# Activation buffers of a two-block network kernel laid out on multiples of 128 bytes in SBUF

## What is computed

```
h = rmsnorm(x, norm1_g[l]) * (1 + sc1) + sh1
x = x + g1 * hybrid_mixer(h, ...)
h = rmsnorm(x, norm2_g[l]) * (1 + sc2) + sh2
x = x + g2 * ((silu(h @ Wg) * (h @ Wu)) @ w_ffn_out[l])
```

## The kernel before, in words

| buffer | used for | begins at (before) | past a multiple of 128 |
|---|---|---|---|
| `weights_hi`, `weights_lo` | stationary operand | 65664, 82048 | 0, 0 |
| `h_hi`, `h_lo` | moving, first block | 107744, 124128 | 96, 96 |
| `rope_cos`, `rope_sin` | VectorE | 140512, 142560 | 96, 96 |
| `o_hi`, `o_lo`, and in their place `hidden_hi`, `hidden_lo` | moving, first block | 145216, 161600 | 64, 64 |
| `y_hi`, `y_lo` | moving, first block | 177984, 194368 | 64, 64 |
| `qk`, `values`, `softmax_buffers` | float32 operands of attention, first block | 182080, 194368, 200512 | 64, 64, 64 |
| `h2_hi`, `h2_lo` | moving (values: stationary), second block | 107232, 131808 | 96, 96 |
| `axial_cos`, `axial_sin` | VectorE | 156384, 158432 | 96, 96 |
| `q2`, `k2`, `hidden2_hi`, `hidden2_lo` | operands, second block | 160896, 173184, 160896, 185472 | 0, 0, 0, 0 |

## Time and profile before

### The profile page before, as it was taken

The page is one execution under the profiler, slowest core; times in us unless marked ns, Lnnn a source line. Parts: engine busy times, 40 slices in busy tenths (PEclk is TensorE's granted clock), DMA queues, the critical chain, the costliest instruction groups (busy, mean ns, idle before and its releaser), DMA issues.

```text
span 3472.7 us, 42728 instructions
## 1 busy us (share of the span) xinstructions
PE 3340.7 (96%) x17614; PEld 2633.1 (76%) x17620; DVE 1268.8 (37%) x2206; ACT 743.4 (21%) x1521; POOL 1584.8 (46%) x996
## 2 busy tenths in 40 slices
PE   6999999999999999999999898999999999899998
PEld 4656777888876667777778786888888888778887
DVE  4843313211258342141122665441111256541113
ACT  2233311100122332110011344220110123431111
POOL 3424466566544244655566322333333343246664
PEclk8999999999999999999999999999999999999999
DMA  6445133333224442245442211132333221123221
GB/s 199 127 155 160 61 96 113 109 87 97 85 91 139 139 139 85 80 145 158 122 128 84 77 37 37 37 100 92 126 122 97 85 76 61 37 82 112 97 97 61
DMA packets 404933, 350.44 MB, mean 101 GB/s; under 512 B 9082, under 2 KB 400890, under 8 KB 404740
## 3 DMA queue, kind: packets, MB, share of 16 engines
q1 hardware_dynamic: 395584, 337.67, 31.2%
q10 hardware_dynamic: 9156, 10.03, 1.0%
HBM read 345.55 MB, written 2.12 MB: 100 GB/s over the span
## 4 chain that ended last, share of the span: by engine, by line
PE 87%; DVE 4%; ACT 2%; POOL 2%; DMA 2%; issue 1%; ACTq 0%; SPq 0%; DVEq 0%; POOLq 0%
PE psum L581 26%; PE psum L583 25%; PE psum L582 25%; PE psum L562 2%; POOL weights_lo L524 2%; DMA raw_weights<-in_w_in 1%; PE psum L969 1%; PE psum L998 1%; PE psum L851 1%; PE psum L818 1%; PE psum L837 1%; PE psum L787 1%; POOL weights_hi L521 1%; PE psum L984 1%; PE psum L649 1%
## 5 line engine op out<-in xcount | busy, mean ns | idle before, releaser
L521 POOL TENSOR_SCALAR weights_hi<-raw_weights 128x1024 fp32r<-128x1024 f32 (+3 forms) x496 | 502.8, 1014 | 1819.6 <-PE psum L583 1509.9
L581 PE MATMUL psum<-h_hi,weights_hi 128*128 128x512 f32 (+1 forms) x2832 | 1128.7, 399 | 41.4 <-DVE h_lo L1856 16.5
L524 POOL TENSOR_TENSOR weights_lo<-raw_weights,weights_hi 128x1024 fp32r<-128x1024 f32 (+3 forms) x496 | 1090.7, 2199 | 41.4
L583 PE MATMUL psum<-h_hi,weights_lo 128*128 128x512 f32 (+1 forms) x2832 | 1075.6, 380 | 0.0
L582 PE MATMUL psum<-h_lo,weights_hi 128*128 128x512 f32 (+1 forms) x2832 | 1071.6, 378 | 0.0
L581 PEld LDWEIGHTS psum<-h_hi,weights_hi 128*128 128x128 f32 x2832 | 536.8, 190 | 198.5 <-issue 56.3
L583 PEld LDWEIGHTS psum<-h_hi,weights_lo 128*128 128x128 f32 x2832 | 536.1, 189 | 110.8
L582 PEld LDWEIGHTS psum<-h_lo,weights_hi 128*128 128x128 f32 x2832 | 537.8, 190 | 104.7 <-issue 9.3
L581 PE MATMUL psum<-hidden_hi,weights_hi 128*128 128x512 f32 (+1 forms) x1120 | 411.2, 367 | 0.0
L582 PE MATMUL psum<-hidden_lo,weights_hi 128*128 128x512 f32 (+1 forms) x1120 | 411.0, 367 | 0.0
L583 PE MATMUL psum<-hidden_hi,weights_lo 128*128 128x512 f32 (+1 forms) x1120 | 410.5, 366 | 0.0
(11 more groups left out here) (261 smaller groups left out, 3336.6 us busy)
## 6 DMA issues: line engine op xcount, KB each, us to landing
raw_weights<-in_ada_w SPq DMA_DIRECT2D x96, 1024.0 KB, 5.3
raw_weights<-in_w_mlp SPq DMA_DIRECT2D x64, 1024.0 KB, 5.2
raw_weights<-in_w_in SPq DMA_DIRECT2D x54, 1024.0 KB, 5.4
raw_weights<-in_w_ffn_in SPq DMA_DIRECT2D x88, 512.0 KB, 5.2
raw_weights<-in_w_out SPq DMA_DIRECT2D x16, 1024.0 KB, 5.0
raw_weights<-in_w_ffn_out SPq DMA_DIRECT2D x16, 1024.0 KB, 5.1
raw_weights<-in_w_in SPq DMA_DIRECT2D x30, 512.0 KB, 5.0
raw_weights<-in_w_branch SPq DMA_DIRECT2D x24, 384.0 KB, 3.0
```

What stands on the lines that cost most here:

```text
L521: gpsimd.tensor_scalar(whi[:, r, c0:c1], raw[:, raw_slot, c0:c1], 1.0, 1.0, ALU.mult, ALU.mult).then_inc(*split_hi.up(*key, half))
L524: gpsimd.tensor_tensor(wlo[:, r, c0:c1], raw[:, raw_slot, c0:c1], whi[:, r, c0:c1].bitcast(F32), ALU.subtract).then_inc(*split.up(*key, half))
L581: tensor.matmul(out, sh, mh, start=first, stop=False, skip_group_check=shared)
L583: return tensor.matmul(out, sl, mh, start=False, stop=last, skip_group_check=shared)
```

## The change

`Map` gets a method that moves its offset up to the next multiple of 128, and three maps use it: before `h_hi` in the first block, before the area that `o`, `hidden`, `y` and the attention buffers share, and before `h2_hi` in the second block. There the three small buffers (`edge_factors`, `softmax_stats_2`, `norm_g2`) are taken first, so that the area behind `axial_sin` still begins at 160896. No instruction is added, removed or moved in the order of any engine, no size changes, and no wait changes; only addresses do.

```diff
+    def align(self):
+
+        self.at = -(-self.at // 128) * 128
+        return self
...
     one = Map(nc, top.at)
     identb = one.take("identity_bf16", [P, P], BF16)
     causal = one.take("causal_bf16", [P, P], BF16)
-    hh = one.take("h_hi", [P, KT, T], F32R)
+    hh = one.align().take("h_hi", [P, KT, T], F32R)
     hl = one.take("h_lo", [P, KT, T], F32R)
...
-    mix = Map(nc, one.at)
+    mix = Map(nc, one.align().at)
     oh = mix.take("o_hi", [P, 8, T], F32R)
...
     two = Map(nc, top.at)
-    gh = two.take("h2_hi", [P, KT, TA], F32R)
-    gl = two.take("h2_lo", [P, KT, TA], F32R)
-    cos2 = two.take("axial_cos", [P, T])
-    sin2 = two.take("axial_sin", [P, T])
     edge = two.take("edge_factors", [P, 4, 16])
     lamr = cst[:, 3:5, :].rearrange("p a (b d) -> p (a b) d", d=HD)
     stat2 = two.take("softmax_stats_2", [P, 4, 8])
     gf2 = two.take("norm_g2", [P, KT])
+    gh = two.align().take("h2_hi", [P, KT, TA], F32R)
+    gl = two.take("h2_lo", [P, KT, TA], F32R)
+    cos2 = two.take("axial_cos", [P, T])
+    sin2 = two.take("axial_sin", [P, T])
```

## The result

| | before | after |
|---|---|---|
| median of 4 runs each, us | 3473.31 (3472.21 to 3477.01) | 3448.62 (3444.55 to 3453.71) |
| ratio, with its 95% interval | | 0.9924 (0.9912 to 0.9936) |
| profiled execution, us | 3474.02 | 3450.2 |
| its span, us | 3472.7 | 3448.9 |

The change is worth 24.7 us. The forecast was 53 us, and 3448.6 lies above the range (3409 to 3445). The sign was right and the size less than half.

What follows compares the result with a forecast made beforehand. TensorE was taken as the bound, by the distance between starts of successive split products. Gains 42.4 + 16.2, less 4.3 and 1.2, made 53 us: 3421.0 for the profiled execution, 3420 us for the median, range 3409 to 3445.

Steps and rivals of the forecast that it cites:

- float32 matmuls and writers: Float32 matmuls of attention and rope, and VectorE and ScalarE writes of hidden parts, get other addresses: no gain, 0.
- The gap rule: N/2.4 + 2.5 ns, 215.8 ns for 512 columns, no address term; supports the no-change rival, 3472 us, chance 0.07.
- step 1: First block: 6528 matmuls of 512 columns moving h, hidden, o, y gain 6.5 ns each, 42.4 us.
- It is an address, but not modulo 128: Rival: class of 1024 or the weights' phase counts; h2 gains, h, o, y, hidden don't; 3458 us, chance 0.06.
- Part of the gain; 3440 to 3450 us: Rival: old offset 64 might leave a rest, or attention give back more than it has; chance 0.05.
- Step 2: Second block: 2496 matmuls moving h2 gain 16.2 us; hidden2 already lies well, 0.
- Step 3: Attention: softmax waits take back part of the 10.9 us gain of 1674 matmuls; 60% kept, minus 4.3 us.
- step 4: Branch boundaries, three in each of two layers: POOL's splitting holds TensorE, 30 matmuls can't gain; minus 1.2 us.
- the signs that the prediction named: Profile after: PE busy down over 50 us, idle up some 5, mainly behind softmax, slightly more POOL wait at branches.
- Step 7: Value tiles, 576 matmuls with h2 stationary: 0, at most 2 us either way.

Runs made afterwards that it cites:

- the first experiment: Kernel after, with h moved 128 bytes and o, y, hidden 256, so all split-product buffers start at 128 modulo 256: 3427.5 us, ratio 0.9868 to the kernel before.

## Why the prediction was right and wrong

**Right.** The bound, and that only durations would change. The price in long runs: 6.5 ns a matmul of 512 columns, nothing to gain for one of 256 (a pair of `h2` became 5.8 ns shorter, less than the 512-column one accounts for by itself), 0 for float32 matmuls and writers. They answer to the earlier trace rows:

```profile
L700 PE MATMUL psum<-qk,constants 128*128 128x512 f32 x24 | 12.3, 592 | 0.0
...
L1016 PE MATMUL psum<-k,constants 128*128 128x512 f32 x16 | 8.3, 598 | 0.0
```

```profile
L2255 DVE TENSOR_TENSOR hidden_lo<-psum,hidden_hi 128x512 fp32r<-128x512 f32 x64 | 44.3, 692 | 31.5 <-ACT hidden_hi L1599 31.5
L2131 DVE TENSOR_TENSOR hidden_lo<-psum,hidden_hi 128x512 fp32r<-128x512 f32 x44 | 30.4, 692 | 28.8 <-ACT hidden_hi L1481 28.8
```

That address is the cause is now shown by kernels that differ in nothing else. The gap rule that the prediction weighed (the Trainium skill, "TensorE: Matmul & The Clock Gate", Back-to-back issue gap) has no term for it and would have given no gain; the measurement decides against it here. The page calls that rule the gap of an isolated matmul and gives some 131 ns for a sustained stream of loads and matmuls at 512 columns. The fastest stream here starts one every 226.7 ns, so neither figure is met.

**The step that failed is step 1**, "First block. Moving operands of 512 columns off a multiple of 128", 42.4 us. It took `h` to gain because its new address is a multiple of 128. What counts is the difference from the weights modulo 256, and that went from 96 to 128, one bad value to another. Without those 4656 matmuls step 1 is 1872 x 6.5 = 12.2 us. Cut at the first value tile, the first block of the profiled executions fell from 1960.2 to 1948.4 us, 11.8; that it comes so close is partly luck, since attention kept some of the gain and the clock differed a little. With the right class, the prediction's own terms give 12.2 + 16.2, less its 1.2 for the branches and 40% of the 4.6 us of `h2` in attention: 25.4 us (an estimate), against 24.7 measured. Where this could have been seen: the earlier trace rows held one buffer at 226.8 ns and two at 233.3. A single cheap example allows any class to which it belongs, and I took the one named in the change. The rival "It is an address, but not modulo 128" had the right mechanism ("the same phase as the weights") and the right verdict on `h`, but a modulus of 1024. So it wrongly gave `o`, `y` and `hidden` (896 modulo 1024, 128 modulo 256) no gain, and came out at 3458. I gave it 0.06, and the text itself said that nothing in the trace separates 128 from 1024. By that sentence it deserved far more, and 256 and 512 should have stood beside it. The rival "Part of the gain; 3440 to 3450 us" (0.05) covers the measured number by luck: it blamed the offset of 64 or the attention stretches, and `hidden` at 64 gained in full once it was moved.

**Step 2** (16.2 us for `h2`): the windows are as forecast. The second block fell from 1512.5 to 1500.5 us, 12.0; with `h2` at the same place in the first experiment it fell to 1497.0, 15.5. The two differ by less than the runs of one kernel do (3444.55 to 3453.71), and the clock can be part of it.

**Steps 3 and 4** (taken off: 4.3 and 1.2 us) can be read against the kernel with everything at 128, where all 9024 matmuls gain: 58.7 us gross, 46.3 measured, so 12.4 were lost, not 5.5. Step 3 is where the size was wrong. I cut the two profiled executions (3472.7 and 3426.9 us, 45.8 apart) into the same stretches. The four that hold attention (before 0:396.1, 1117.8:1330.6, 1960.2:2335.4 and 2857.3:3151.3) have 2520 of the 9024 matmuls, 16.4 us at 6.5 ns, and became 4.5 us shorter together: 11.9 us lost. All the rest has 6504, 42.3 us, and became 41.3 us shorter. Most of the loss, 7.0 us, is in the first of them, the first layer up to its first branch product. Its 840 matmuls should have gained 5.5 us, and it became 1.5 us longer:

```profile
0.00:396.10 396.10, 352.00 (x2117) 239.01 (x2120) 209.77 (x496) 126.92 (x299) 134.57 (x96) 0.96 0.47 146
```

```profile
0.00:397.60 397.60, 353.74 (x2120) 240.91 (x2120) 206.91 (x496) 127.00 (x299) 135.08 (x96) 0.95 0.46 145
```

Part of this is the clock: by the clock records of the traces 31.8 us there ran at half speed before and 37.5 us with everything at 128, which is worth at most 2.9 us (an estimate). For the rest two things can be shown. The first is short runs. This is the attention stretch of the first block's second layer, up to its first branch product, before and with everything at 128:

```profile
1117.80:1330.60 212.80, 198.69 (x1357) 131.40 (x1360) 84.27 (x228) 83.50 (x227) 60.73 (x44) 0.99 0.41 128
```

```profile
1103.50:1316.30 212.80, 198.37 (x1361) 131.40 (x1361) 84.14 (x228) 83.71 (x227) 60.66 (x44) 0.99 0.41 128
```

It holds some 430 split products, which at 6.5 ns would be 2.8 us, and it did not get shorter by anything. PE's busy time fell by 0.3. The products come there mostly in runs of three to nine between small matmuls. From a small matmul through nine products to the next one, before and with everything at 128, start and duration in us:

```profile
1201.35 0.38 PE L837 MATMUL psum<-constants,softmax_buffers 128*128 128x128 f32 x2
1201.48 0.48 PE L581 MATMUL psum<-h_hi,weights_hi 128*128 128x512 f32 x1
...
1203.67 0.38 PE L837 MATMUL psum<-constants,softmax_buffers 128*128 128x128 f32 x2
```

```profile
1187.16 0.38 PE L844 MATMUL psum<-constants,softmax_buffers 128*128 128x128 f32 x2
1187.29 0.48 PE L588 MATMUL psum<-h_hi,weights_hi 128*128 128x512 f32 x1
...
1189.46 0.38 PE L844 MATMUL psum<-constants,softmax_buffers 128*128 128x128 f32 x2
```

2.32 against 2.30 us: some 2 ns a matmul instead of 6.5. The full gain came only in long unbroken runs, and what little was gained between waits the waits took back. The prediction took 6.5 ns for each of them and let 60% of the attention's part stand.

The second is POOL, by waits that grew. PE's waits for it, before, after, and with everything at 128 (total us, times, longest):

```profile
PE psum L581 <- POOL weights_lo L524: 15.8, 19, 2.4
```

```profile
PE psum L586 <- POOL weights_lo L529: 22.2, 23, 2.6
```

```profile
PE psum L588 <- POOL weights_lo L531: 23.5, 23, 3.1
```

The branches give 1.2 of the 7.7 us between the first and the third (0.5 to 1.1 us in each layer), just what step 4 said. But the prediction looked only there. The rest came at the start of the first layer (1.3), after `y` (1.9), in the attention of the second layer (0.5), and most of all in that of the last block's last layer (2.2 to 5.0 us). My reading, which was followed only at the branches: where a split starts only when an earlier product frees the buffer, its 3.5 us are fixed and PE merely gets to them sooner. In the last place it can't be told from the clock what the wait cost: that stretch fell from 294.0 to 289.9 us, all that its 624 matmuls had to give, but at a granted clock of 0.97 before and 0.99 with everything at 128.

The page agrees with the sum. With everything at 128, PE's busy time is 50.4 us below before, 8.3 less than the 58.7, and its idle time 4.6 above:

```profile
PE 3290.3 (96%) x17620; PEld 2629.9 (77%) x17620; DVE 1268.7 (37%) x2206; ACT 743.7 (22%) x1521; POOL 1586.3 (46%) x996
```

So the signs that the prediction named (PE busy down by more than 50, idle up by some 5) came out in this kernel, which is what it believed the change to be.

**Step 7** (stationary `h2`, at most 2 us either way) held, with a loss. 144 of their matmuls, in the last layer, before and after:

```profile
2857.28:2874.35 17.07, 17.07 (x146) 16.93 (x145) 9.92 (x14) 3.23 (x8) 6.75 (x4) 1.00 0.25 78
```

```profile
2838.72:2856.16 17.44, 17.44 (x146) 17.31 (x146) 9.92 (x14) 3.23 (x8) 6.75 (x4) 1.00 0.25 77
```

0.37 us more in the quarter of them that this is, 2.6 ns each, so a loss of some 1.5 us in all if the others are alike (an estimate). They take 121 ns from start to start in this row and some 118 before. With 256 columns and the weights moving, the same start modulo 256 is no help and even costs a little.

## What to carry to other kernels

Where products with a pair of high and low operands fill TensorE, place the moving buffers at the same offset modulo 256 bytes as the weight buffers, high and low parts alike; the offset itself doesn't matter. Measure it from start to start in unbroken runs, more than one of them, since the same buffers can show several rhythms. Mean durations give it only in part: before the change L581 took 395 ns on `hidden` (338.9 less 199.9 us over 352) and 390 on `hidden2`, 5 ns apart instead of 6.5. Count the gain only for long runs. When one cheap case and a few dear ones suggest a rule for addresses, write down every modulus and every difference that fits them before choosing, and give each a chance.

## What the runs showed of the hardware that was not expected

- A split product of 512 columns starts every 226.7 ns when the starts of its moving and stationary operands are equal modulo 256, wherever that is (0, 128 and 192 were tried). It takes 233.3 ns at differences of 32, 96, 192 and 224, and some 234 at 160. At 128 it takes 233.3 ns in some stretches and 232.4 to 232.6 in others (`h2` and `hidden2` with the weights at 0; `h` in the gate tiles of the kernel after).
- A difference of 64 gives 228.9 ns, or 233.3 in other chunks of the same kernel.
- The cost is not each matmul's own. Only the low moving part off: 228.9, 231.1 or 233.3 ns by stretch; only the high one off, 229.0; only the low weights off, 231.1. The mechanism is open. No run changed the order of the three matmuls or the distance between successive k tiles.
- In runs of nine products between small matmuls the gain was some 2 ns a matmul instead of 6.5.
- Matmuls of 256 columns with `h2` moving and the float32 ones of this kernel show no such price. Those of 256 columns with `h2` stationary became slower at an equal start, by 2.6 ns in the row above.
